# Gate products of an RG-LRU as two 64-row tiles, moved between the halves of the next projection

## What is computed

```python
xc = conv4(u) + conv_b                      # causal, per channel, 512 channels
xb = xc.reshape(B, T, 8, 64)                # 8 blocks of 64 channels
r = sigmoid(einsum("bthi,hij->bthj", xb, w_gate_a) + b_gate_a)
i = sigmoid(einsum("bthi,hij->bthj", xb, w_gate_x) + b_gate_x)
log_a = -8 * r * softplus(-lru_lambda)
a = exp(log_a); b = sqrt(-expm1(2 * log_a)) * (i * xc)
h[t] = a[t] * h[t-1] + b[t];  y = h * gelu(gate_in)
```

## Time and profile before

| | |
|---|---|
| median of 3 runs | 1151.81 us (1150.91 to 1152.33) |
| the profiled execution, its own time | 1152.54 us |
| its span from first to last instruction | 1150.7 us |
| PE busy | 1124.6 us (98%) |
| DVE busy | 785.9 us (68%) |
| ACT busy | 399.6 us (35%) |

### The profile page before, as it was taken

The page is one execution under the profiler, slowest core; times in us unless marked ns, Lnnn a source line. Parts: engine busy times, 40 slices in busy tenths (PEclk is TensorE's granted clock), DMA queues, the critical chain, the costliest instruction groups (busy, mean ns, idle before and its releaser), DMA issues.

```text
span 1150.7 us, 14008 instructions
## 1 busy us (share of the span) xinstructions
PE 1124.6 (98%) x5110; PEld 909.0 (79%) x5110; DVE 785.9 (68%) x1127; ACT 399.6 (35%) x728; POOL 52.2 (5%) x94
## 2 busy tenths in 40 slices
PE   7999999999989999999999999999999999999996
PEld 6888887677656788878888888888888888888885
DVE  6666765756577546888867667766766766766768
ACT  7433932545467336642212112212221211211222
POOL 0300001001011110000000000000000000000010
PEclk9999999999999999999999999999999999999998
DMA  6111423111100455111111021110211102012162
GB/s 230 56 37 36 136 84 100 48 37 42 33 19 19 148 190 193 73 39 72 37 73 36 36 73 36 46 64 36 73 36 41 68 36 73 36 36 73 37 234 113
DMA packets 23397, 83.11 MB, mean 72 GB/s; under 512 B 3088, under 2 KB 3216, under 8 KB 23232
## 3 DMA queue, kind: packets, MB, share of 16 engines
q1 hardware_dynamic: 17424, 62.92, 15.4%
q0 software_dynamic: 5648, 19.60, 5.0%
q10 hardware_dynamic: 288, 0.09, 0.0%
HBM read 70.02 MB, written 8.39 MB: 68 GB/s over the span
## 4 chain that ended last, share of the span: by engine, by line
PE 89%; DVE 5%; DMA 2%; ACT 1%; issue 1%; SPq 0%; DVEq 0%; ACTq 0%
PE pair L352 27%; PE pair L354 27%; PE pair L353 27%; PE pair L725 3%; PE pair L760 2%; DMA raw<-weights 2%; PE pair L742 1%; DVE negmax L1657 1%; DVE y_gain L2087 1%; PE pair L728 1%; PE pair L574 1%; DVE yacc L2072 1%; DVE h_sb L2101 1%; DVE wl L1478 0%; PE pair L771 0%
## 5 line engine op out<-in xcount | busy, mean ns | idle before, releaser
L354 PE MATMUL pair<-wdh,xl 128*128 128x512 f32 x480 | 186.7, 389 | 0.0
L352 PE MATMUL pair<-wdh,xh 128*128 128x512 f32 x480 | 186.7, 389 | 0.0
L353 PE MATMUL pair<-wdl,xh 128*128 128x512 f32 x480 | 186.7, 389 | 0.0
L1883 DVE TENSOR_TENSOR yacc<-yacc,pair 128x1024 f32<-128x1024 f32 x104 | 127.0, 1221 | 80.3 <-PE pair L354 80.3
L1378 ACT ACTIVATE up_h<-raw 128x384 fp32r<-128x384 f32 x56 | 27.4, 513 | 227.8 <-DMA raw<-weights 227.8
L352 PEld LDWEIGHTS pair<-wdh,xh 128*128 128x128 f32 x480 | 90.1, 188 | 18.7
L353 PEld LDWEIGHTS pair<-wdl,xh 128*128 128x128 f32 x480 | 90.1, 188 | 18.7
L354 PEld LDWEIGHTS pair<-wdh,xl 128*128 128x128 f32 x480 | 90.1, 188 | 18.7
L352 PE MATMUL pair<-xh,wh 128*128 128x512 f32 x256 | 102.1, 399 | 1.0 <-DVE xl L1501 1.0
L354 PE MATMUL pair<-xh,wl 128*128 128x512 f32 x256 | 99.9, 390 | 0.0
L353 PE MATMUL pair<-xl,wh 128*128 128x512 f32 x256 | 99.7, 389 | 0.0
(11 more groups left out here) (305 smaller groups left out, 2100.3 us busy)
## 6 DMA issues: line engine op xcount, KB each, us to landing
raw<-weights SPq DMA_DIRECT2D x74, 512.0 KB, 3.4
wd_f<-weights SPq DMA_DIRECT2D x28, 512.0 KB, 3.6
x_sb<-x SPq DMA_DIRECT2D x8, 512.0 KB, 7.6
q_rot<-q_sb POOLq DMA_DIRECT2D x32, 128.0 KB, 2.8
out<-h_sb POOLq DMA_DIRECT2D x8, 512.0 KB, 3.4
h_sb<-out POOLq DMA_DIRECT2D x8, 512.0 KB, 11.2
out<-h_sb SPq DMA_DIRECT2D x7, 512.0 KB, 2.6
x_a<-x POOLq DMA_DIRECT2D x4, 512.0 KB, 6.9
```

The lines of the kernel that those rows point to most:

```text
L352: pe.matmul(o, a_hi, b_hi, start=first, stop=False)
L353: pe.matmul(o, a_hi, b_lo, start=False, stop=False)
L354: return pe.matmul(o, a_lo, b_hi, start=False, stop=last)
L1883: dve.tensor_tensor(y, y, pair[2 + t % 2][:, :], ALU.add).then_inc(y_added, 1)
```

## The change

The gate matrices are no longer block diagonal. A 128 x 128 matrix per chunk now holds, in its rows 0 to 63, the two gates of the first block side by side, and in rows 64 to 127 those of the second block. A matmul takes 64 rows: the first block's result goes to pair 2 and the second's to pair 3, and the two follow each other in the program. There are again 12 matmuls in a chunk. The results of the two gates now lie in halves of two pairs, so ACT applies four sigmoids of 64 partitions in place of two of 128.

The gate products of chunks 1 and 2 move behind the first half of the u piece of the next chunk; those of the last chunk move into the middle of token piece 8 (after 12 of its 24 matmuls). PE's loop over chunks 2 and 3 is written out. On DVE, the low half of the next u weights moves ahead of the convolution in all chunks (before, only in chunk 0). The halves of piece 10 move up: on ACT ahead of gelu's sigmoid of the last chunk, on DVE ahead of the products that follow the chunks.

```diff
@@ gate_products(c), PE
                 pe.wait_ge(xc_lo, c + 1)
-                for g in range(2):
-                    for hf in range(2):
-                        tok = slice(HALF * hf, HALF * hf + HALF)
-                        mm = mm3(pe, pair[2 + g][:, tok], gwh[:, g, :], gwl[:, g, :], xch[:, tok],
-                                 xcl[:, tok], True, True)
-                    mm.then_inc(gates_done, 1)
+                for hf in range(2):
+                    tok = slice(HALF * hf, HALF * hf + HALF)
+                    for n, (w, u) in enumerate(((gwh, xch), (gwh, xcl), (gwl, xch))):
+                        for g, rows in enumerate((slice(0, 64), slice(64, P))):
+                            mm = pe.matmul(pair[2 + g][:, tok], w[rows, :], u[rows, tok], start=n == 0, stop=n == 2)
+                            if n == 2:
+                                mm.then_inc(gates_done, 1)
@@ chunks and token pieces, PE
-            gate_products(1)
-            with pe.Fori(2, LC) as c:
+            for c in range(2, LC):
                 for s in range(2):
                     pe.wait_ge(w_lo, 2 * c + s + 1)
-                    for mm in feature_piece(s, pair[s], xh, xl):
-                        pass
+                    for hf, mm in enumerate(feature_piece(s, pair[s], xh, xl)):
+                        if (s, hf) == (0, 0):
+                            gate_products(c - 1)
                     mm.then_inc(piece_used, 1)
-                gate_products(c)
...
-                    token_piece(j % 2, j, range(4 * half, 4 * half + 4), 4 * half)
+                    if p == P_VA:
+                        token_piece(0, 0, range(4), 0, parts=(0,))
+                        gate_products(LC - 1)
+                        token_piece(0, 0, range(4), 0, parts=(1,))
+                    else:
+                        token_piece(j % 2, j, range(4 * half, 4 * half + 4), 4 * half)
@@ chunks, ACT
-                act.activation(gwh[:, :, :], gw_raw[:, c, :, :], ACT.Copy)
+                act.activation(gwh[:, :], gw_raw[:, c, :], ACT.Copy)
...
-                act.wait_ge(gates_done, 2 * c + 1)
-                act.activation(dec[:, c, :], pair[2][:, :], ACT.Sigmoid,
-                               bias=cols[:, bass.ds(c + C_BA, 1)]).then_inc(sig_done, 1)
-                act.wait_ge(gates_done, 2 * c + 2)
+                act.wait_ge(gates_done, 4 * c + 4)
+                act.activation(dec[0:64, c, :], pair[2][0:64, :], ACT.Sigmoid,
+                               bias=cols[0:64, bass.ds(c + C_BA, 1)]).then_inc(sig_done, 1)
+                act.activation(dec[64:P, c, :], pair[3][64:P, :], ACT.Sigmoid,
+                               bias=cols[64:P, bass.ds(c + C_BA, 1)]).then_inc(sig_done, 1)
                 act.wait_ge(ix_done, c)
-                act.activation(lru_a[:, :], pair[3][:, :], ACT.Sigmoid,
-                               bias=cols[:, bass.ds(c + C_BX, 1)]).then_inc(sig_done, 1)
+                act.activation(lru_a[0:64, :], pair[2][64:P, :], ACT.Sigmoid,
+                               bias=cols[0:64, bass.ds(c + C_BX, 1)]).then_inc(sig_done, 1)
+                act.activation(lru_a[64:P, :], pair[3][0:64, :], ACT.Sigmoid,
+                               bias=cols[64:P, bass.ds(c + C_BX, 1)]).then_inc(sig_done, 1)
+                if c == LC - 1:
+                    hi_early(P_VA + 2)
...
-                if c < 2:
-                    hi_early(P_VA + 2 + c)
+                if c == 1:
+                    hi_early(P_VA + 3)
@@ recurrent(c, first) and after it, DVE
-                if first:
-                    lo(wl[0][:, :], wh[0][:, :], 0, 3)
+                lo(wl[0][:, :], wh[0][:, :], 0, 2 * c + 3)
...
-                dve.tensor_tensor(gwl[:, :, :], gw_raw[:, c, :, :], gwh[:, :, :].bitcast(F32), ALU.subtract)
+                dve.tensor_tensor(gwl[:, :], gw_raw[:, c, :], gwh[:, :].bitcast(F32), ALU.subtract)
...
-                if not first:
-                    lo(wl[0][:, :], wh[0][:, :], 0, 2 * c + 3)
...
+            lo_early(P_VA + 2)
...
-                if c < 2:
-                    lo_early(P_VA + 2 + c)
+                if c == 1:
+                    lo_early(P_VA + 3)
@@ lay_out_gates(wa, wx)
+    g = np.empty((P, LC, P), np.float32)
+    for c in range(LC):
+        g[0:64, c, 0:64], g[0:64, c, 64:P] = wa[2 * c], wx[2 * c]
+        g[64:P, c, 0:64], g[64:P, c, 64:P] = wx[2 * c + 1], wa[2 * c + 1]
```

More of the change, by code:

```diff
@@ L116, in build @@
         lru_g = sb("lru_g", [P, T], F32, at_s + 12 * KB)
-        gwh = sb("gwh", [P, 2, P], F32R, at_s + 16 * KB)
-        gwl = sb("gwl", [P, 2, P], F32R, at_s + 17 * KB)
+        gwh = sb("gwh", [P, P], F32R, at_s + 16 * KB)
+        gwl = sb("gwl", [P, P], F32R, at_s + 17 * KB)
         cos_t = sb("cos_t", [P, 2, T], F32, at_s)
@@ L189, in build @@
         hrstd = small("hrstd", [P, 32])
-        gw_raw = sb("gw_raw", [P, LC, 2, P], F32, at_v)
+        gw_raw = sb("gw_raw", [P, LC, P], F32, at_v)
         lam_raw = sb("lam_raw", [P, 4, 64], F32, at_s + 18 * KB)
@@ L511, in _ @@
             pool.wait_ge(squares_v, 2)
-            pool.dma_start(gw_raw[:, :, :, :], gate_weights).then_inc(gates_loaded, 16)
+            pool.dma_start(gw_raw[:, :, :], gate_weights).then_inc(gates_loaded, 16)
             links = [0]
@@ L536, in _ @@
             nc.gpsimd.tensor_scalar(spl[:, 1, :], acc, -LRU_C, None, ALU.mult).then_inc(spl_ready, 1)
-            pool.wait_ge(gates_done, 2 * LC)
+            pool.wait_ge(gates_done, 4 * LC)
             pool.dma_start(cos_t[:, :, :], rope).then_inc(rope_loaded, 16)
@@ L672, in _ @@
                 else:
-                    pe.wait_ge(sig_done, 2 * LC)
+                    pe.wait_ge(sig_done, 4 * LC)
                 for j in range(N_V):
@@ L1117, in _ @@
                 hi(None, wh[1][:, :], (piece_used, 2 * c + 2, 1, 16 * c + 32))
-                act.wait_ge(gates_done, 2 * c + 1)
-                act.activation(dec[:, c, :], pair[2][:, :], ACT.Sigmoid,
-                               bias=cols[:, bass.ds(c + C_BA, 1)]).then_inc(sig_done, 1)
-                act.wait_ge(gates_done, 2 * c + 2)
-                act.wait_ge(ix_done, c)
-                act.activation(lru_a[:, :], pair[3][:, :], ACT.Sigmoid,
-                               bias=cols[:, bass.ds(c + C_BX, 1)]).then_inc(sig_done, 1)
+                act.wait_ge(gates_done, 4 * c + 4)
[3 more added lines that the diff above has]
+                               bias=cols[64:P, bass.ds(c + C_BA, 1)]).then_inc(sig_done, 1)
+                act.wait_ge(ix_done, c)
+                act.activation(lru_a[0:64, :], pair[2][64:P, :], ACT.Sigmoid,
[4 more added lines that the diff above has]
+                    hi_early(P_VA + 2)
                 act.wait_ge(gelu_in, c + 1)
                 act.activation(lru_g[:, :], lru_g[:, :], ACT.Sigmoid, scale=GELU_S).then_inc(gelu_sig, 1)
-                act.wait_ge(sig_done, 2 * c + 2)
+                act.wait_ge(sig_done, 4 * c + 4)
                 if c == 0:
@@ L1587, in recurrent @@
                 lo(wl[1][:, :], wh[1][:, :], 1, 2 * c + 4)
-                dve.wait_ge(sig_done, 2 * c + 2)
+                dve.wait_ge(sig_done, 4 * c + 4)
                 dve.tensor_tensor(xc_t[:, c, :], xc_t[:, c, :], lru_a[:, :], ALU.mult).then_inc(ix_done, 1)
```

## The result

The changed kernel takes 1154.59 us (median of 10 runs, 1153.73 to 1156.06) against 1152.07 us for the kernel before in the same session (10 runs, 1150.82 to 1154.46). The ratio is 1.002, with an interval of 1.0012 to 1.0029: 2.5 us or 0.22% slower (1.4 to 3.3 us by the interval), a small change that can just be told from none. The forecast was 1152.8 us. The profiled execution took 1153.97 us, its span is 1152.2 us, 1.5 us more than before.

What follows compares the result with a forecast made beforehand. PE was taken to set the pace, with ACT and DVE nearly level; 3.84 us saved on PE against 4.8 us of waits made + 1.0 us, so 1152.8 us; own range 1151.2 to 1154.6, 8-in-10 range 1150.8 to 1154.7.

Steps and rivals of the forecast that it cites:

- rival (b): New idle PE time before the token pieces lowers PE's clock: half speed for 3.3 us, + 2.7 us, 1154.5 us; chance 0.13.
- the sum: Whole stage of token pieces: 3.84 us saved on PE, 4.8 us lost in waits, + 1.0 us on the span.
- no change: Whole kernel: forecast of 1152.8 us, within the 0.2% (2.3 us) counted as indistinguishable; chance 0.76.
- The tiled group: One chunk's gate products on PE: 6 x 0.227 + 0.40 = 1.76 us instead of 2.72, pairs overlapping in full.
- Rival (a): Gate pairs on PE do not overlap in fp32r: 1.36 us more per group, + 6.4 us, 1158.2 us; chance 0.06.
- its 0.20 and 0.11 us: Leaving a tiled group on PE: 0.20 for an unhidden weight load and way out, 0.11 for the first full-array load behind.
- The bank wait: Before the first token piece, PE stalls 1.9 us, to 112.86 us, until DVE has scaled the last g piece.
- rival (c): ACT or DVE quicker than assumed, saving comes through: - 0.7 to - 4 us; chance 0.05 for more than 0.2% faster.
- the sigmoids' spacing: ACT's four 64-partition sigmoids per chunk at 1.00 us each: 4.00 us instead of 2.00.
- bound of 1.10 us a sigmoid: Upper case for ACT's sigmoids in the forecast's own range: 0.8 us more.
- The waits at pieces 10 and 11: PE waits for DVE's low halves before these token pieces: 0.5 and 1.3 us, 1.8 together.
- small steps at pieces 12 to 16: Forecast for pieces 13 to 16: PE waits 1.1 us in steps of 0.3, at 5.44 us a piece against DVE's 5.72.

Runs made afterwards that it cites:

- the kernel just above: Changed kernel, but last chunk with block-diagonal gates and two sigmoids, gates behind two token tiles, piece 10's high half behind the last tanh: 1149.63 us, 0.9978 of the kernel before.
- the kernel with the filled wait: Changed kernel plus eight unused full-array matmuls while PE waits for the scaling of g before the first token piece: 1153.81 us, 1.0015 of the kernel before.
- the kernel with the split wait: Changed kernel, but PE waits for the scaling of g only before the third token tile: 1152.66 us, 1.0008 of the kernel before.

## Why the prediction was nearly right

The mechanism was as forecast: a wait before the token pieces, a full queue behind it, and more lost in waits than saved. The size was not. The forecast moves the time by 1.0 us, below the 1.4 to 3.3 us of the interval; the median of 1154.59 us lies 1.8 us above the forecast, and only 0.1 us below the upper end of its range, 1154.7, which had been drawn to take in rival (b). Of the 1.8 us, 0.3 lies in the kernel before, whose median beside the changed kernel was 1152.07 and not 1151.81 us, 0.7 in a queue longer than forecast, and the rest, by estimate, in the clock, which the sum puts at nothing. That the range held, and that the slowdown passes for the forecast's "no change" (0.22% against its 0.2%), is in part luck.

- **The tiled group** (forecast 1.76 us) takes 1.79. Rival (a), no overlap in fp32r, fell. Without losses at the edges a group would take 6 x 0.227 = 1.36 us, so the edges cost 0.43, about half going in and half coming out. The loss comes with the tiles: in the kernel just above, the last gates, on the full array, go in and out without it, 112.41 + 2.72 = 115.13 us. What the 0.43 us is made of is not shown, and the weight loads that the forecast names in its 0.20 and 0.11 us are its author's estimate; behind each of the changed kernel's three waits, too, the second matmul starts 0.31 to 0.34 us after the first, 0.1 us later than usual.
- **The bank wait** (forecast 1.9 us, PE at 112.86) is 1.94 us idle, PE at 113.20. The forecast's 1.9 counts from the moment when PE is due; counted so, from 110.87 + 0.227 = 111.10, it is 2.1 us. Of the 1.94 us, 1.45 are the bare way over DVE's scaling and stay even if DVE is never late, as the kernel with two sigmoids shows. The forecast had this in rival (c), with 1.5 us, but its main account puts the whole wait down to DVE's queue.
- **The term of the sum that was mis-sized is the sigmoids' spacing**, "I take 1.00, since a lane's 1024 elements stay". It is 1.14, because neighbours that write different partitions do not overlap (1.12 us apart where the partitions change in the kernel with the sigmoids in another order, 1.02 and 1.01 where they stay, at 1.10 to 1.11 us each), so a chunk costs 0.55 us more. With 0.22 us by which the last sigmoids start later than forecast (117.82 against 117.60) it makes 0.77, and the first square root is 138.58 - 137.87 = 0.71 us late. From there all is passed on as forecast: low half of piece 16 at 161.82 against 161.12, q projection at 161.88 against 161.2, 1.7 us later than before instead of 1.0. The forecast's own bound of 1.10 us a sigmoid was on the right side and too low.
- **The waits at pieces 10 and 11** (forecast 0.5 and 1.3 us) are 0.69 and 0.98 us of idle time, or 0.85 and 1.14 from the moment when PE is due (the matmuls before them start at 125.74 and 132.19 us): 2.0 us against 1.8. With the bank wait's 2.1, some 0.3 for the slow restarts and about 1.0 in small steps at pieces 12 to 16, PE loses 5.4 us and not 4.8.
- **Rival (b), the clock**, got 0.13 and was stated as all or nothing. Its 1.7 us is the lost half of the 3.3 us at clock 0.50 that the earlier trace rows show at 314 us, behind the 1.74 us of idle PE of the earlier trace rows. It happens in a part of the executions: it costs 1.6 us where it does, and adds to the queue instead of replacing it. The queue alone is 1.55 us of the median, by the kernel with the filled wait; the changed kernel beside it was 1155.26 - 1153.81 = 1.45 us above that. The intervals of the two ratios overlap (1.0006 to 1.0023, 1.0013 to 1.0034), so the size is not settled. That there is such a part is shown by the 79 of 88 pairs and by the two profiles, and the kernel with the split wait agrees: its median is 2.6 us under the changed kernel's, and the queue explains 1.4 of them. An estimate is 1 us of the 2.5.
- **Rival (c)**, a quicker ACT or group, fell on both counts: 1.14 us and 1.79 us.
- **The sum**: PE saved 4 x 0.93 = 3.7 us, and the stage ended 1.7 us later. Two things gave that back and more, and each was undone alone: the four sigmoids (2.4 us of span) and the last gates' place (2.3 us). They hit the same queue, so they are not to be added.

## What to carry to other kernels

Where PE, ACT and DVE are nearly level, price a saving on PE together with what it adds on ACT: tiling split each result over two buffers and doubled ACT's passes, each as long as before (1.11 us). Use such a saving only where the other engines have room (here chunks 0 to 2), and leave something on PE between a buffer's last matmul and its next use, to cover the way over DVE and back (1.45 us here). A wait such as the 1.94 us here, in a dense stream of matmuls, must be priced twice, once for itself and once for the slower clock that may follow (0.50 for 3.4 us in one of the changed kernel's two profiled executions).

## What the runs showed of the hardware

- The two matmuls of a pair of row tiles in fp32r start 1 to 5 ns apart by their single records, and pairs follow at 0.23 us (changed kernel), where single full-array matmuls follow at 0.227: the two of a pair overlap in full.
- An ACT pass over 64 partitions from PSUM takes 1.11 us for 1024 columns (changed kernel, last chunk), where one over 128 takes 1.09 to 1.12 (kernel before, two sigmoids). Successive passes start 1.00 to 1.02 us apart where they write the same partitions (kernel before, two sigmoids, sigmoids in another order), 1.12 to 1.14 where they write different ones (changed kernel, sigmoids in another order).
- PE's granted clock went to 0.50 behind 1.84 and 3.24 us of idle time between dense matmuls in the kernel with tiles and no moves, and behind 1.94 us in one execution of the changed kernel; the windows at 0.50 are 3.2 to 3.4 us long. Behind the 1.94 us this cost 1.6 us. Behind the same 1.94 us it stayed at 1.00 in another execution, as it did in the profiles with 1.45 us of idle time (two sigmoids, moves without tiles).
